# An eight-core encoder trunk: stores and a square sum issued later in the attention stages, one product on GpSimd, other filling rates, borrowed weight tiles

## What is computed

```
# layer 0
proj = rmsnorm(h) @ w_in                       # latents of mixer A, q k v of mixer B
o_mla = attention(8 heads, dq 96, dv 64)       # mixer A
w = softmax(q1 k1) - lam * softmax(q2 k2)      # mixer B, 4 heads, two 64-wide parts each
o_d = rmsnorm(w @ v) * (1 - lam_init)          # the sub-layer norm, over 128 values
h = h + concat(o_mla, o_d) @ w_out
h = h + (silu(n @ w_gate) * (n @ w_up)) @ w_down,  n = rmsnorm(h), hidden 2816
# layer 1
q, k, v = rmsnorm(h) @ w_qkv ; q, k = axial_rope(rmsnorm per head)   # 8 q heads, 2 kv heads, 128 wide
h = h + attention(q, k, v) @ w_out
h = h + swiglu(rmsnorm(h))
return rmsnorm(h)
```

## Time and profile before

| what | value |
|---|---|
| three runs, median | 6154.4 us (6142.96 to 6551.47) |
| the profiled execution's own time | 6154.84 us |
| its span (slowest core, core 6) | 6153.3 us; the others 6123.3 to 6144.2 |
| TensorE (PE) busy | 5707.0 us, 93% |
| weight loads (PEld) | 2420.2 us |
| VectorE (DVE) | 3026.8 us, 49% |
| ScalarE (ACT) | 4137.1 us, 67% |
| GpSimd (POOL) | 832.3 us, 14% |

### The profile page before, as it was taken

How to read it: one execution, slowest core, us unless ns; L and a number is a source line. 1 busy time by engine, 2 the same in 40 slices (tenths; PEclk the granted TensorE clock), 3 DMA queues, 4 the chain that set the end, 5 groups by cost and what they waited for, 6 DMA issues and landing times. The chain is left out here.

```text
span 6153.3 us, 97205 instructions; the slowest of 8 cores (6123.3 to 6153.3 us)
## 1 busy us (share of the span) xinstructions
PE 5707.0 (93%) x28020; PEld 2420.2 (39%) x28568; DVE 3026.8 (49%) x4184; ACT 4137.1 (67%) x6667; POOL 832.3 (14%) x928
## 2 busy tenths in 40 slices
PE   5789999997999999999999988799999999999998
PEld 1234444442334344444444433334344444444443
DVE  4633333333555556565656555344444444444443
ACT  3479999997776767676767653386766666666641
POOL 2423324200102020202020211200000000000000
PEclk8799999998999999999999999899999999999999
DMA  5557557504334343434343424412222322223234
GB/s 152 139 154 227 169 147 223 155 18 96 85 107 124 110 126 121 128 121 131 120 127 122 129 96 143 128 46 79 77 94 90 102 95 89 96 90 106 87 104 143
DMA packets 314091, 722.51 MB, mean 117 GB/s; under 512 B 41072, under 2 KB 101744, under 8 KB 307952
## 3 DMA queue, kind: packets, MB, share of 16 engines
q1 hardware_dynamic: 304112, 689.72, 37.1%
q0 software_dynamic: 9472, 26.55, 1.6%
HBM read 596.40 MB, written 125.30 MB: 117 GB/s over the span
## 5 line engine op out<-in xcount | busy, mean ns | idle before, releaser
L203 ACT ACTIVATE P<-S 128x512 bf16<-128x512 f32 (+1 forms) x5120 | 3287.3, 691 | 1157.6 <-PE S L197 1010.4
L197 PE MATMUL S<-Qt,Kt 128*128 128x512 bf16 (+1 forms) x5955 | 2108.9, 382 | 97.5 <-ACT P L203 34.5
L197 PE MATMUL O<-P,Vt 128*128 128x512 bf16 x6038 | 2145.7, 381 | 28.8 <-DVE os L223 9.1
L197 PE MATMUL F<-hn,wgu 128*128 128x512 bf16 x5525 | 1442.8, 380 | 39.0 <-DMA wgu<-gu 12.3
L197 PEld LDWEIGHTS S<-Qt,Kt 128*128 128x128 bf16 (+1 forms) x6144 | 597.7, 98 | 1096.1 <-issue 580.3
L197 PEld LDWEIGHTS O<-P,Vt 128*128 128x128 bf16 x6144 | 600.8, 98 | 666.4 <-issue 39.3
L197 PEld LDWEIGHTS F<-hn,wgu 128*128 128x128 bf16 x5632 | 549.4, 98 | 680.8 <-issue 48.7
L197 PE MATMUL F<-ac,wdn 128*128 128x512 bf16 x2751 | 711.5, 381 | 30.9 <-DMA wdn<-dn 23.7
L226 DVE RECIPROCAL rc<-lc 32x128 f32<-32x128 f32 x512 | 480.8, 939 | 42.1 <-DVE rc L226 1.8
L208 DVE TENSOR_TENSOR hb<-hb,F 128x512 f32<-128x512 f32 x256 | 175.5, 685 | 617.0 <-PE F L197 613.7
L197 PEld LDWEIGHTS F<-ac,wdn 128*128 128x128 bf16 x2816 | 275.3, 98 | 355.5 <-issue 40.1
(11 more groups left out here) (118 smaller groups left out, 4540.3 us busy)
## 6 DMA issues: line engine op xcount, KB each, us to landing
wgu<-gu SPq DMA_DIRECT2D x352, 512.0 KB, 3.7
wf<-w_gu SPq DMA_DIRECT2D x44, 1024.0 KB, 9.3
wdn<-dn SPq DMA_DIRECT2D x128, 352.0 KB, 3.9
wdn<-dn SPq DMA_DIRECT2D x64, 704.0 KB, 4.2
Kt<-kd SPq DMA_DIRECT2D x128, 256.0 KB, 6.8
Vt<-vd SPq DMA_DIRECT2D x128, 256.0 KB, 6.8
gu<-wb SPq DMA_DIRECT2D x44, 512.0 KB, 6.3
wf<-w_dn SPq DMA_DIRECT2D x32, 704.0 KB, 6.9
```

Of the source, the lines that this page charges most:

```text
L197: self.S.op("tensor", lambda e: e.matmul(out, lhsT=lhsT, rhs=rhs, start=start, stop=stop), reads, writes)
L203: self.S.op("scalar", lambda e: e.activation(out=out, in_=in_, func=func, scale=scale), reads, writes)
```

## The change

Seven edits: the DMA semaphores go from 40 to 48. `Stream` is written anew and fills all its tiles at the start; later it asks for a tile when it did before, and can be given more tiles. `attend` takes 5 units of other work after each closing step that is due after the last job. The rates go from 2.95 to 2.84 and from 2.5 to 2.42. The last product of SiLU in `stage_b` is issued on GpSimd. The stores of q, k and v are put into chains, and so are issued at the fourth tick (v: third and fourth). `var` comes three steps later, and `store` and `follow` with it. After the last job of `stage_b`, pieces of the K and V tiles are lent to the streams: 4 tiles for `wdn`, 3 for `wsm`, 2 for `wgu`; their DMAs wait for the last readers of K and V.

```
-    def __init__(self, nc, stack, n_dma_sems=40, n_sw_sems=30):
+    def __init__(self, nc, stack, n_dma_sems=48, n_sw_sems=30):
...
     def begin(self):
+        while self.idle and self.srcs:
+            t = self.idle.popleft()
+            self.kb.dma("sync", t.t[:], self.srcs.popleft(), (), [t.b], t.b)
+            self.ready.append(t)
+
+    def add(self, tiles):
+        self.idle.extend(tiles)
+        self.begin()
 
     def next(self):
+        if self.cur is not None:
+            self.idle.append(self.cur)
+        self.begin()
+        self.cur = self.ready.popleft()
+        return self.cur
+
+def borrow(tile, view, name):
+
+    t = Tl(view, name)
+    for c in [tile.b] + tile.cb:
+        for o in [c.last_w] + list(c.readers.values()):
+            if o is not None:
+                t.b.readers[("before", id(o))] = o
+    return t
...
     for i in sorted(due):
         for fn in due[i]:
             fn()
+        behind.pull(5)
...
-    attend(jobs, behind, lambda job: 2.5 if job.j else 0.0)
+    attend(jobs, behind, lambda job: 2.42 if job.j else 0.0)
...
-            lambda: kb.tt("vector", ac.t[:, m, :], g.t[:], e.t[:], ALU.mult, [g.b, e.b], [ac.cb[m]]))
+            lambda: kb.tt("gpsimd", ac.t[:, m, :], g.t[:], e.t[:], ALU.mult, [g.b, e.b], [ac.cb[m]]))
...
-            kb.dma("sync", dst, qo.t[:], [qo.b], (), qo.b)
+            behind.chain(lambda: None, lambda: None, lambda: None, lambda: kb.dma("sync", dst, qo.t[:], [qo.b], (), qo.b))
...
-        for i in range(2):
-            kb.dma("sync", vgv[i][:, j * 4:j * 4 + 4, :], vst.t[:, :, i * 128:(i + 1) * 128], [vst.b], (), vst.b)
+        def store(i):
+            return lambda: kb.dma("sync", vgv[i][:, j * 4:j * 4 + 4, :], vst.t[:, :, i * 128:(i + 1) * 128], [vst.b], (), vst.b)
+
+        behind.chain(lambda: None, lambda: None, store(0), store(1))
...
-            return steps + [mix] + [lambda: None] * 4 + [var, lambda: None, store]
+            return steps + [mix] + [lambda: None] * 7 + [var, lambda: None, store]
...
-    attend(jobs, behind, lambda job: 2.95 if job.j else 0.0, cuts=(12, 20, 32))
+    attend(jobs, behind, lambda job: 2.84 if job.j else 0.0, cuts=(12, 20, 32))
...
+    wdn.add(pieces(Kts[0], "xdn", 2, HD) + pieces(Vts[0], "xdn", 2, HD))
+    wsm.add(pieces(Kts[1], "xsm", 3, 8))
+    flat = Vts[1].t[:].rearrange("p j c -> p (j c)")
+    wgu.add([borrow(Vts[1], flat[:, i * 2048:(i + 1) * 2048].rearrange("p (a k c) -> p a k c", a=2, k=8), "xgu") for i in range(2)])
     behind.drain()
```

More of the change, by code:

```diff
@@ L256, in __init__ @@
     def __init__(self, kb, tiles, srcs):
-        self.kb, self.tiles, self.srcs = kb, tiles, srcs
-        self.used = 0
-        self.begun = False
+        self.kb, self.srcs = kb, collections.deque(srcs)
+        self.idle = collections.deque(tiles)
+        self.ready = collections.deque()
+        self.cur = None
     def begin(self):
[L262 to L268, removed]
-    def next(self):
[L271 to L277, removed]
+        while self.idle and self.srcs:
[5 more added lines that the diff above has]
+        self.begin()
+    def next(self):
+        if self.cur is not None:
[10 more added lines that the diff above has]
+    return t
 class Behind:
@@ L1005, in stage_b, with pieces @@
     kb.load_w(None, w_v, Wv, Wv.b, 8, 1280, 1536)
-    attend(jobs, behind, lambda job: 2.95 if job.j else 0.0, cuts=(12, 20, 32))
+    attend(jobs, behind, lambda job: 2.84 if job.j else 0.0, cuts=(12, 20, 32))
+    def pieces(tile, name, n, k):
+        flat = tile.t[:] if len(tile.t[:].shape) == 2 else tile.t[:].rearrange("p j c -> p (j c)")
+        return [borrow(tile, flat[:, i * k * 128:(i + 1) * k * 128].rearrange("p (k c) -> p k c", k=k), name) for i in range(n)]
+    wdn.add(pieces(Kts[0], "xdn", 2, HD) + pieces(Vts[0], "xdn", 2, HD))
+    wsm.add(pieces(Kts[1], "xsm", 3, 8))
+    flat = Vts[1].t[:].rearrange("p j c -> p (j c)")
+    wgu.add([borrow(Vts[1], flat[:, i * 2048:(i + 1) * 2048].rearrange("p (a k c) -> p a k c", a=2, k=8), "xgu") for i in range(2)])
     behind.drain()
```

## The result

The changed kernel takes 6096.6 us in the median, before it was 6154.4: ratio 0.9914, 95% interval 0.9893 to 0.9936. By the ratio that is 53 us or 0.9% less (39 to 66 by its interval; the medians lie 57.8 apart), about 60% of the 87 us forecast. It is inside the wide range of 6022 to 6115 and inside the 2% that were called the same, but outside the forecast's own range of 6040 to 6092. Its profiled execution took 6115.31 us, with a span of 6113.8 on core 5 and 6054.7 to 6098.6 on the others.

A forecast was written before the change was run, and what follows sets the result against it. TensorE sets the time, so its waits and low-clock stretches can be won: 12.5 + 14.4 + 3.5 + 34.5 + 18 + 4 = 87 us off, to 6067 us (1.4% faster), own range 6040 to 6092, wide range 6022 to 6115.

The forecast's parts named there:

- The rates: Block boundaries of `stage_b`: lower rates leave fewer empty steps, 2.5 us at each of 5 blocks, 12.5 us, bounds 7 and 20.
- `var`: Attention part of `stage_b`: three steps later removes six long sqd waits, 2.4 us each, 14.4 us, bounds 7 and 20.
- The stores: Attention part of `stage_b`: stores four ticks later no longer hold up SP, so the wsm<-oo waits go, 3.5 us.
- No edit touches that: Attention part of `stage_b`: wdn waits behind the next head's K and V (16.3 us) stay, 0 us, bounds -5 and +20.
- The rival for more gain: "More goes than was counted": K and V shift off wdn loads, reciprocal waits shrink, boundaries reach 20; 6027 us, chance 0.2.
- (a): Start of `stage_b`'s tail: left-over work covers the 12.5 us sqd wait; borrowed loads before `wsm` cost about 3; 10 us gained.
- (c): `gate_up(7)` in `stage_b`'s tail: fewer wgu waits with four tiles, and the ring from 4.04 to 3.93 us; 5.5 us.
- (d): Tail of `stage_b`: the wdn waits go with seven tiles, 7 us, clock included.
- `stage_c`, 18 and 4 forecast: Six boundaries lose most of the wait for `at`, 18 us (10 to 20); in the tail 22 units go under it, 4.
- the last rival: "The GpSimd product slows DVE": each product meets a clamp or closing copy, 144 us more, 6211 us, chance 0.05.
- Half stays hidden: Rival: boundaries give 7, sqd rest drops the clock, the `at` wait half stays, tail gives 13; 6111 us, chance 0.2.
- the signs set beforehand: Right: no sqd wait over 0.5 us, `stage_b` tail clock above 0.95, length near 320; wrong: new PE waits for wk or POOL.

## Why the prediction was right, and where it was not

The change made the kernel faster by less than 2%, as forecast, but part of that is luck. The time fell outside the forecast's own range and nearer to the rival of 6111 us than to 6067, and errors of opposite sign met in one stretch. The forecast counted losses, so the measured gains are compared without the work that only moved (8.4 us in `stage_b`, 3.4 in `stage_c`).

*Attention part of `stage_b`, 30 forecast, 15 measured, an estimated 6.5 without the moved work.* Most of what is missing is missing here. Three terms stand in it.

- The rates, 12.5: without the burst 11.5 were measured, but 5.8 of them are moved work. The 5.7 that are left lie below the term's bounds of 7 and 20, and over both stretches the rates are worth 2.7. The boundary was sized too large, at 2.5 us for each of five blocks where 1.1 came; why is open.
- `var`, 14.4: the job with `var` came to 18.38 us (18.5 forecast), the wait is gone without a rest, and without the burst the edit is worth 15.7, or 13.3 without the moved work. Right as to the wait, and near in size, with waits for wk that rose by 18 us and others that fell in the balance; what failed is that I took a job of block 0, which has no filler, for all it does. In blocks 1 to 7 the same edit moves the filler three steps, and in the kernel before this gave nearly everything back (3 of 18 us left).
- The stores, 3.5: measured 20.6 in this kernel, with a scatter of 8.5. The term was sized by the waits visible before, where only `wsm<-oo` was late. Behind a burst the same hold-up of SP adds 19 us of waits for `wsm<-qk`.

The step that failed is "No edit touches that", on the 2 MB of K and V in front of a `wdn` load, with "the load still falls into the down projection". I asked only where the known stall would go. It did shrink, from 16.3 to 3.9 us on the cores shown (11.8 to 5.0 in the mean); but the burst then met `wsm` and `wgu` loads, whose waits rose by 12.8 and 9.7 us in the mean. Waits for wk rose by 9.5 on top; the prediction named them only as a sign of being wrong. The rival for more gain had seen that the phase takes K and V off the wdn loads and stopped there.

So two errors of opposite sign met: the stores gave some 17 us more than they were credited with, and the phase took back more than that. How much more can't be added up, as the terms change with the burst.

*Tail of `stage_b`, 34.5 forecast, 23.4 measured, an estimated 31.8 without the moved work.* In size this is near. (a), put at 10, I trusted least. The wait for sqd is 5.5 us and not 0: I had let 12.5 us of matmuls cover a chain of DVE that stays 12 us long, but the pulled groups stretch it, from the copy of os at 3626.07 to the end of sqd at 3647.53, 21 us. The 3 us for "the bulk of borrowed loads" measured 3.6 in the median of the cores (7.06 on the slowest), but the load that was late was tg, not `wsm`. (c) the ring of 3.93 us was right to 0.01. In (c) and (d) I gave the tiles some 3 and 7 us: without them the tail is as long, so nothing of its gain is theirs. The pulls are worth 6.3; the lower rates cost 8.8, of which 5.8 are the moved work; the stores are worth 3 while the tiles are there. How the rest divides is not settled.

*`stage_c`, 18 and 4 forecast.* The attention part gave 17.9, and the version with old rates gave it back to 0.3 us; 3.4 of it is moved work, so that 14.5 stand against 18. No weight tile was late there. The tail was to win 4 and lost 3, all of it the 16 moved matmuls (3.4 us): the pulled groups were put under the wait for `at`, but they lengthened the chain behind it from 10 to 12.7 us, and the wait only fell from 8.30 to 7.55.

*The product on GpSimd.* The prediction took from the Trainium skill, SBUF — State Buffer, "Who interferes with whom", that an instruction of VectorE with two SBUF inputs contends with GpSimd. The trace agrees: squares of 692 ns take 1579 when they meet a product. A copy that meets one takes 1157, where the last rival had 1240, but 13 of 192 copies do and none of the clamps, so that its 144 us did not come.

*Rivals.* "Half stays hidden" (6111) is 14 us from 6096.6, the forecast (6067) 30. Its boundaries (7) are nearer to what the rates left than my 12.5, and its tail had the borrowed loads delay the start and DVE hold the pace, both of which the traces show, though not as 22 us less. Its sqd rest and its half of the waits for `at` did not come. The largest loss, the new waits for weights in the attention part, is in no rival. Of the signs set beforehand, those for the tail failed (clock 0.94 and not above 0.95, 333 us and not near 320, a wait for sqd of 5.5), and one of the wrong ones came, new waits for wk.

## What to carry to other kernels

A wait that goes from the trace is a gain only if what moves along with it meets nothing else: when an edit shifts a stream of small loads against a periodic burst on the same queue, redo the burst's position against every stream, not only the one that waits today. Better, take the burst out first (worth 46 us in the changed kernel, by one piece per eight steps), and then measure the other edits; the later `var` came near its forecast only without it. Count the work in each stretch before its time is called a gain: what an edit leaves for a later stretch shortens the earlier one. Extra buffers for a stage that is held by an engine's ring win nothing, and filling them delays the small load behind. To see whether two engines disturb each other, compare the instructions that overlap with those that don't; a median over all of them shows nothing when few meet.

## What the runs showed that was not expected

- The delay of a load behind 2 MB: 256 KB tiles that land in 3.3 us in the median took 10.4 and 9.3, and with PE's waits of up to 7.8 us the job's clock was 0.93 and not 1.00, so that a job of 38.0 us took 47.6.
- Rates and burst don't add: lowering the rate by 4% was worth 11.5 us of the attention part in one case and 25 in the other, 2.7 and 16 together with the tail.
- What remains in the version with pieces is 25.8 us of waits for wk, 15 of up to 1.9 us: the matmuls over the squares of q and k wait for a rotation on DVE that stands behind a reciprocal or a copy of rc. Before it was 7.3 in the mean; nothing was tried against it.
- The product on GpSimd slows what it meets on VectorE: an rc copy from 419 to 1157 ns, a square from 692 to 1579.
